# Newton steps with per-partition scalars, and the first gate tile of each z group with its high weight parts ahead of its low ones

## The reference

```
x = x + rms_norm(merged @ w_mix_out, g_post_mix)          # after attention and a state-space branch
x = x + rms_norm(memory_cross_attention(rms_norm(x, g_pre_xa), rms_norm(mem, g_mem), ...), g_post_xa)
x = x + rms_norm(swiglu(rms_norm(x, g_pre_ffn), w_gu, w_down), g_post_ffn)
...
x = x + gate1 * mixed                                     # second block: window attention and gated linear attention
x = x + gate2 * peer_ffn(rms_norm(x) * (1 + scale2) + shift2, ...)   # experts' rows gathered by top-k
return rms_norm(x)

rms_norm(x, g) = x * rsqrt(mean(x * x) + 1e-6) * g
```

## Time and profile before

| what | us |
|---|---|
| median of 3 runs (2932.72 to 2933.24) | 2932.98 |
| the profiled execution, its own time | 2932.72 |
| its span, first to last instruction | 2931.0 |
| TensorE busy | 2715.8 (93%) |
| DVE busy | 1660.7 (57%) |
| POOL busy | 1365.0 (47%) |
| ACT busy | 926.0 (32%) |

### The profile page before, as it was taken

How to read it: one execution, slowest core, us unless ns; L and a number is a source line. 1 busy time by engine, 2 the same in 40 slices (tenths; PEclk the granted TensorE clock), 3 DMA queues, 4 the chain that set the end, 5 groups by cost and what they waited for, 6 DMA issues and landing times.

```text
span 2931.0 us, 32370 instructions
## 1 busy us (share of the span) xinstructions
PE 2715.8 (93%) x12050; PEld 2054.9 (70%) x12050; DVE 1660.7 (57%) x3133; ACT 926.0 (32%) x1646; POOL 1365.0 (47%) x1003
## 2 busy tenths in 40 slices
PE   8989999899998889999897799999999999999944
PEld 7856888767887678888776678888888754434411
DVE  1032145476245254330306659999895999856686
ACT  3275343665233342332335232111112930000001
POOL 4422543665455133444342336444445954544465
PEclk9999999999999999999999899999999999999978
DMA  5311232332243136654230138999999279999998
GB/s 167 109 44 37 85 103 87 122 98 82 90 144 119 51 113 200 207 179 105 74 105 1 52 132 290 384 393 394 371 391 406 81 262 386 390 411 409 409 385 306
DMA packets 219373, 598.85 MB, mean 204 GB/s; under 512 B 22337, under 2 KB 47314, under 8 KB 218834
## 3 DMA queue, kind: packets, MB, share of 16 engines
q1 hardware_dynamic: 135280, 300.70, 30.0%
q0 software_dynamic: 75968, 275.81, 24.9%
q10 hardware_dynamic: 7970, 20.28, 2.1%
HBM read 584.84 MB, written 7.41 MB: 202 GB/s over the span
## 4 chain that ended last, share of the span: by engine, by line
PE 70%; DVE 12%; DMA 9%; POOL 4%; issue 3%; ACT 2%; DVEq 0%; ACTq 0%; SPq 0%; POOLq 0%
PE ps L1807 15%; PE ps L1305 13%; PE ps L1306 13%; PE ps L1307 13%; DMA rows<-in_v,expert 5%; DMA rows<-in_u,expert 4%; DVE ps L2511 3%; POOL rows L1216 2%; PE ps L1271 1%; POOL wlo L1094 1%; PE ps L1404 1%; PE ps L1835 1%; DVE rows L2497 1%; PE ps L1491 1%; PE ps L1493 1%
## 5 line engine op out<-in xcount | busy, mean ns | idle before, releaser
L1094 POOL TENSOR_TENSOR wlo<-wraw,whi 128x1024 fp32r<-128x1024 f32 x258 | 627.9, 2444 | 804.4 <-ACT whi L583 790.2
L583 ACT ACTIVATE whi<-wraw 128x1024 fp32r<-128x1024 f32 x258 | 269.7, 1058 | 690.0 <-PE ps L1307 589.2
L1847 PE MATMUL ps<-stream,hg 128*128 128x512 f32 x1024 | 443.1, 596 | 7.1 <-DMA stream<-in_v 7.1
L1807 PE MATMUL ps<-haff,stream 128*128 128x256 f32 x2048 | 444.1, 380 | 2.2 <-ACT stg L998 2.2
L1305 PE MATMUL ps<-hhi,whi 128*128 128x512 f32 x1088 | 426.8, 392 | 11.8 <-DVE hlo L1972 4.8
L1807 PEld LDWEIGHTS ps<-haff,stream 128*128 128x128 f32 x2048 | 390.1, 191 | 55.7 <-ACT stg L998 2.4
L1307 PE MATMUL ps<-hhi,wlo 128*128 128x512 f32 x1088 | 424.1, 390 | 0.0
L1306 PE MATMUL ps<-hlo,whi 128*128 128x512 f32 x1088 | 423.9, 390 | 0.0
L1216 POOL DMA_INDIRECT rows<-in_u,expert x256 | 268.8, 1050 | 261.5 <-DVE hid L2497 134.7
L1847 PEld LDWEIGHTS ps<-stream,hg 128*128 128x128 f32 x1024 | 195.5, 191 | 254.5 <-issue 245.9
L1216 POOL DMA_INDIRECT rows<-in_v,expert x256 | 250.6, 979 | 256.5 <-DVE ps L2511 122.9
(11 more groups left out here) (463 smaller groups left out, 4395.3 us busy)
## 6 DMA issues: line engine op xcount, KB each, us to landing
stream<-in_ut SPq DMA_DIRECT2D x128, 512.0 KB, 6.7
stream<-in_v SPq DMA_DIRECT2D x128, 512.0 KB, 6.8
wraw<-in_w_in SPq DMA_DIRECT2D x96, 512.0 KB, 3.7
wraw<-in_w_ada SPq DMA_DIRECT2D x48, 512.0 KB, 4.0
wraw<-in_w_gu SPq DMA_DIRECT2D x88, 256.0 KB, 3.8
wraw<-in_w_down SPq DMA_DIRECT2D x22, 512.0 KB, 3.5
decs<-acs_kept ACTq DMA_DIRECT2D x16, 512.0 KB, 3.7
wraw<-in_w_br_ssm SPq DMA_DIRECT2D x16, 512.0 KB, 3.5
```

The source lines that it names most:

```text
L583: act.activation(whi[:, n % WSLOTS, 0:kn, :], wraw[:, n % WSLOTS, 0:kn, :], ACT.Copy).then_inc(w_hi, 1)
L1094: pool.tensor_tensor(wlo[:, n % WSLOTS, 0:kn, :], wraw[:, n % WSLOTS, 0:kn, :], whi[:, n % WSLOTS, 0:kn, :].bitcast(F32), ALU.subtract).th ...
L1807: ins = pe.matmul(ps[:, n % 2, 0:ND], stream[j][:, k, :], haff2[:, 1, k, :], start=k == 0, stop=k == KD - 1)
L1847: ins = pe.matmul(ps[:, 2 * i + half, :], hg[:, n, P * i:P * i + P], stream[j][:, 4 * half:4 * half + 4, :], start=n == 0, stop=n == NKEYS ...
```

## The change

In `z_tile` the first token tile (j = 0) of a z group waits for the high part of a chunk alone and does the two products that need only high weights, for all four chunks; then it waits for the low parts and does the third product, again for all four chunks. The other three tiles are as before. In `newton` two `scalar_tensor_tensor` instructions become `tensor_scalar` ones: what was read as a second tensor of one column is read as a scalar for each partition. The arithmetic is the same.

```diff
 # z_tile
+                if j == 0:
+                    for n in range(first, last + 1):
+                        _, k0, kn, _ = CHUNKS[n]
+                        pe.wait_ge(w_hi, plain_before[n + 1])
+                        for kk in range(kn):
+                            pe.matmul(dst, hhi[:, k0 + kk, t], whi[:, n % WSLOTS, kk, :], start=k0 + kk == 0, stop=False)
+                            pe.matmul(dst, hlo[:, k0 + kk, t], whi[:, n % WSLOTS, kk, :], start=False, stop=False)
+                    for n in range(first, last + 1):
+                        _, k0, kn, _ = CHUNKS[n]
+                        pe.wait_ge(w_lo, plain_before[n + 1])
+                        for kk in range(kn):
+                            ins = pe.matmul(dst, hhi[:, k0 + kk, t], wlo[:, n % WSLOTS, kk, :], start=False, stop=k0 + kk == KD - 1)
+                    ins.then_inc(acc_ready, 1)
+                    return
                 for n in range(first, last + 1):
                     _, k0, kn, _ = CHUNKS[n]
-                    if j == 0:
-                        pe.wait_ge(w_hi, plain_before[n + 1])
-                        pe.wait_ge(w_lo, plain_before[n + 1])
 # newton
-                link(v.scalar_tensor_tensor(t[:, c], y[:, c], mid[:, c], y[:, c], ALU.mult, ALU.mult))
-                link(v.scalar_tensor_tensor(dst[:, c], t[:, c], 3.0, y[:, c], ALU.subtract, ALU.mult))
+                link(v.tensor_scalar(t[:, c], y[:, c], mid[:, c], y[:, c], ALU.mult, ALU.mult))
+                link(v.tensor_scalar(dst[:, c], t[:, c], 3.0, y[:, c], ALU.subtract, ALU.mult))
```

More of the change, by code:

```diff
@@ L1482, in z_tile @@
                     pe.wait_ge(s("btok_ready"), u + 1)
+                dst = ps[:, 2 + u % 2, :]
+                if j == 0:
[12 more added lines that the diff above has]
+                    return
                 for n in range(first, last + 1):
                     _, k0, kn, _ = CHUNKS[n]
-                    if j == 0:
-                        pe.wait_ge(w_hi, plain_before[n + 1])
-                        pe.wait_ge(w_lo, plain_before[n + 1])
                     for kk in range(kn):
                         k = k0 + kk
-                        dst = ps[:, 2 + u % 2, :]
                         pe.matmul(dst, hhi[:, k, t], whi[:, n % WSLOTS, kk, :], start=k == 0, stop=False)
```

## The result

| | before | after |
|---|---|---|
| median, 7 runs each, us | 2933.14 (2928.97 to 2935.13) | 2941.89 (2939.03 to 2944.20) |
| profiled execution, span, us | 2931.0 | 2940.2 |
| mean granted clock of TensorE | 0.972 | 0.965 |

The kernel became slower: 1.003 times the time before, 95% interval 1.0020 to 1.0039, some 9 us. The forecast of 2923.0 was wrong by 19 us and the time lies outside the range. What came is the rival that had 0.04: the clock falls at the z changes. The Newton lines did in round 1 nearly what was forecast.

What follows compares the result with a forecast made beforehand. TensorE was taken to bound the kernel (70% of the chain, busy 93%). Z tiles -1.3, round 0 +0.4, round 1 -6.5 and -2.0, rounds 2 and 3 -0.5, round 4 +0.1: -9.8 from 2932.72, so 2923.0 us, range 2920.5 to 2928.5.

Steps and rivals of the forecast that it cites:

- the rival that had 0.04: Slower: at the z changes TensorE's clock falls behind 2.3 us idle; 2939.5 with low stretches of about 11 us; chance 0.04.
- the clock at the z changes: TensorE idle 2.3 us in one piece at each z change, near the 2.2 us passed at 883 without a fall.
- a sign of being wrong: Lines 1907 or 1908 still showing 2 us, transposes waiting for other than ACT's copies, or low clock over z matmuls.
- the rival's milder case: Clock low 6.8 us at each z change, costing 3.4 us each, 10.2 for three, giving 2933.2; counted as same.
- The z edit's own worth: Two matmuls instead of six after the last low part; 0.44 us gained at each z change, 1.3 for three.
- The price of the new lines: New line 1907 at 0.28 us, or 0.214 at least, 1908 at 0.214; about 0.1 more per call, round 0 +0.4.
- Not held: The new Newton lines are not held by POOL's subtractions, no instruction over 0.3 us; the held rival had chance 0.08.
- Round 1, first part: Each u_added needs one POOL turn, the last ending near 876.8, not 880.45; xv0 starts 2.2 us earlier.
- the bet that was called even: Whether DVE's first line 1939 in round 1 comes behind POOL's start; if so only 1.1 of 2.2 us is won.
- Round 1, second part, and the clock there: x_scaled end near 896, ACT late next; transposes 6.5 us earlier, 4.3 from this part; clock stays up, another 2.0.
- Rounds 2 and 3: One held line 1907 in each: 0.35 us less, 0.1 back for the last call, so 0.25 gained per round.
- gains carry to the end: Later steps are TensorE's own work without waits, so gains carry on; the whole sum of -9.8 us reaches the end.

Runs made afterwards that it cites:

- e1: The kernel before with only the z_tile part of the diff, old Newton lines; median 2941.31 us, ratio 1.0028 to before.
- e4: The kernel after with 5 and 9 unread matmuls filling TensorE's two idle pieces at each z change, 42 in all; 2929.40 us, ratio 0.9987 to before.
- e9: The kernel after with only the 9 unread matmuls ahead of the fourth chunk's low part at each z change; 2929.64 us, ratio 0.9987 to before.
- e3: The kernel before with the new Newton lines and the new z order for the last chunk alone; 2930.06 us, ratio 0.9986 to before.
- e8: The kernel before, old Newton lines, with 8 extra matmuls at the start of xq1; 2933.92 us, ratio 1.0004 to before.
- e12: The kernel before with the new Newton lines for x_scaled only, z as before; 2930.40 us, ratio 0.9987 to before.
- e10: The kernel after with only the 5 unread matmuls ahead of the third chunk's low part at each z change; 2930.58 us, ratio 0.9990 to before.
- e5: The kernel before, unchanged, measured and traced a second time; 2933.49 us, ratio 1.0002 to before.
- e11: The kernel before with the new Newton lines for u_added only, z as before; 2935.83 us, ratio 1.0007 to before.
- e6: e2 with 7 extra matmuls, some 1.6 us, at the start of xq1; 2929.92 us, ratio 0.9988 to before.
- e7: e3 with 5 extra matmuls, 1.1 us, at the start of xq1; 2927.50 us, ratio 0.9979 to before.
- e2: The kernel before with only the two new Newton lines, z tiles as before; 2929.83 us, ratio 0.9978 to before.

## Why the prediction was wrong, step by step

**The step that failed: the clock at the z changes.** The prediction counted the idle 2.3 us as harmless because 2.2 us had passed without a fall at 883, and gave the fall 0.04. The fall came, 6.8, 10.2 and 10.2 us long, and cost 9.2 us net; a low clock over z matmuls is what the prediction itself had named as a sign of being wrong. Shown by e1 (slower by itself), e4 and e9 (more work, no fall, 12.5 and 12.2 us shorter than after) and e3 (same order of the last chunk, short pieces, no fall). Two things were misread. First, one passing of such an idle time was taken as a property of the chip, but in the same place, behind the same wait of 2.04 us, e1, e8 and e12 fell: the row was luck. Second, the new order makes two pieces, 0.8 and 2.0 us, not one of 2.3, since TensorE waits for the third low part too, and each step that had separated the waits in the earlier trace rows (six matmuls) shrank to two.

**The rival's price** was nearly right by place: 2.3 us net at a stretch of 6.8, 3.4 and 3.5 at those of 10.2; with the edit's own 0.3 added back, 2.6 and 3.7 to 3.8, where it had 3.4 for each 6.8 us (5.1 for 10.2). Part of a stretch costs nothing: at the second change its first 1.0 us is still idle, up to the last low part at 619.2, and the wait of 0.38 for DVE's mask product disappears. The sum is 9.2 net, where the rival's milder case had 10.2, or 8.9 net of its 1.3 for the z edit, and was read as undoing the rest (2933.2). The other 8.7 us up to 2941.9 are for the most part the gains that were forecast and did not last, below.

**The z edit's own worth.** Forecast 0.44 at each change, measured 0.34 to 0.40 in e3 and 0.29 to 0.34 in e4, with the wait for DVE behind it as described. Right where the clock lets it.

**The price of the new lines.** Forecast 0.28 and 0.214; measured 0.273 and 0.214. Together 0.11 more per call than 0.220 and 0.159. Round 0: from the start of its first line 1912 to that of its last line 1916, 5.13 us before and 5.55 after, +0.42 for +0.4.

**Not held.** Right: none of the 64 took over 0.276 us, and 18 of them ran while POOL was busy; before, 13 of the 64 took over 0.3. The Trainium skill (SBUF — State Buffer, "Who interferes with whom") says that a DVE instruction with at most one SBUF input, outside its two-port modes, does not contend with GpSimd. The trace agrees, if the scalars for each partition are not counted as such inputs: 0.276 us at most. In which mode the new lines ran no trace shows.

**Round 1, first part.** Forecast 2.2 of xv0's wait, measured 1.3 (2.04 to 0.74). It is the bet that was called even and was lost: POOL started at 875.07 like DVE's line 1950, which took 3.49. By the prediction that leaves 1.1. The last `u_added` ended at 888.61, which is 1.3 earlier than before once the 9.5 of the z changes is taken off, for 3.6 in the forecast.

**Round 1, second part, and the clock there.** Idle time ahead of the transposes 6.06 to 1.75, so 4.3 as forecast; ACT's copies of vx late next, as forecast; 32 transposes in 3.7 for 5.7 us, so 2.0 as forecast. Round 1 in all: 7.6 for 8.5, the difference being the lost bet. That the clock stays up there was right in this trace and not in each: in e10 it fell behind 1.86. And part of the forecast gain is luck of the trace it started from: in the short course of e8, with old lines, 2.8 were left to win.

**Rounds 2 and 3.** Forecast 0.25 won in each; won were 0.35 and 0.66, by the same DVE instructions on either side. Too small to matter.

**The second failure: that gains carry to the end.** The sum assumed that nothing behind round 1 changes but by its own edit. It does. After gives back 1.7 near 970 and 4.1 between 1447 and 1600, with the clock low at 969.8, 1444.2 and 1451.0, and in a third stretch of 3.4 us between 1567 and 1598 where the kernel before has two. Of the 4.1, 2.8 are lost by 1470 and 1.4 between 1560 and 1570. e5, the same code as before, shows none of it; e1, with old Newton lines, has both (1.7 and 4.3), and e8, with old lines too, and e11, with old ones in `x_scaled`, the second (4.3 each; e8's 1.8 ahead of it are its eight extra matmuls). So it is not a cost of the new lines. That it goes with where in time the work comes to lie is not shown: counted from the start of the span, e11's work at 1430 lies 0.3 us ahead of before's, between two traces of the unchanged kernel (0 and 1.2 ahead) that lose nothing, and e11 loses 4.3. The cause stays open: the shift in e6 removed the stretch at 959 and not those at 1434 and 1440; e7 and e12 gave back only 1.3 and 1.4 of the 4.3.

**The parts do not add up.** e1 is 7.3 us above its kernel before, e2 4.2 below it: 3.1 by the sum, +8.8 by the measurement (by the ratios 1.8, give or take some 4). In the traces, e1 had itself taken a short course in round 1 (4.8), so that the Newton lines had only 2.8 left to win there, and after lost 7.3 behind round 1 where e1 lost 5.1.

**Left open:** which course each run without a trace took, which gap of idle time is enough for a fall, and why the later stretches sit where they do.

## What to carry to other kernels

Small waits between bursts of matmuls can be worth keeping: an order that gathers them into pieces of some 0.8 and 2 us close together can cost more in clock than it wins in waits, and splitting only the last chunk took the same 0.4 us at each change without it (e3). Against the Newton lines alone (0.9978, with e7 at 0.9979 the fastest) that gain was too small to see in the time. One row that shows the clock staying up through such an idle time is one draw; look for it in a second trace before building on it. And where TensorE bounds a kernel, compare the granted clock stage by stage behind the edit too, since low stretches far behind an edit can differ from one version to the next, by some 4 us here, as much as the edit wins.

## What the runs showed of the hardware

- The same wait of 2.04 us ahead of xv0 left the clock at 2.4 GHz in two traces (before, e5) and was followed by 3.4 us at 1.2 GHz in three others (e1, e8, e12); the same wait of 2.18 us ahead of the attention was followed by 3.4 us at 1.2 GHz in seven traces of 14.
- Idle pieces of 0.8 and 2.0 us with two matmuls between them were followed by 6.8 or 10.2 us at 1.2 GHz at six changes of six, although at the first TensorE was busy for 9.86 of the 12.7 us up to 577.7; with nine unread matmuls in the second piece it stayed at 2.4 GHz at three changes of three.
- A 128 x 1 `tensor_scalar` takes 0.146 us with immediates, 0.214 with one scalar for each partition, 0.273 with two; beside POOL's subtractions the last stayed under 0.28. A 128 x 1 instruction with two tensor inputs takes 0.16 or 0.22 alone and up to 2.3 us beside POOL, and in e8 0.16 when it came in a pause of 0.48 us.
- A stretch of low clock need not make a stage longer: e8 and e1, with old Newton lines and 3.4 us at half clock in round 1, have two pauses of 0.48 us on POOL, and their round 1 is 4.8 us shorter than that of before.
